# Gated linear recurrence heads: level decays as in-place products of blocks, heads interleaved

## The chip, the core and the metric

The kernel runs on one core of one Trainium2 chip. Time is the device time of one execution in microseconds (us). TensorE (PE) multiplies matrices, VectorE (DVE) does elementwise work and reductions, ScalarE (ACT) functions by table and copies, GpSimd (POOL) further elementwise work, and SyncE (SP) issues loads. Each engine runs its own program, and they meet only at semaphores. On-chip memory is SBUF; matmuls write PSUM, 8 banks of 128 partitions x 512 f32.

## The reference

A trunk of two layers, width 1024, 1024 tokens. Layer 0 has two mixers side by side, an S5 state space model with a gated linear unit (GLU) and an HGRN2 recurrence of 4 heads; layer 1 has sliding window attention. Each layer ends in an MLP and a gated embedding. The change is in the HGRN2 heads alone:

```python
log_f = jnp.logaddexp(jnp.log(jnp.maximum(lbf, 1e-30)),
                      jnp.log1p(-lbf) + jax.nn.log_sigmoid(zf))
k = (1.0 - lbf) * jax.nn.sigmoid(-zf)
...
def step(S, xs):                      # chunks of 64 tokens, 4 heads
    q_c, k_c, v_c, g_c = xs           # g_c is log_f
    b = jnp.cumsum(g_c, axis=2)
    o_inter = jnp.einsum('bhtk,bhkv->bhtv', q_c * jnp.exp(b), S)
    diff = b[:, :, :, None, :] - b[:, :, None, :, :]
    decay = jnp.exp(jnp.where(causal[None, None, :, :, None], diff, -jnp.inf))
    att = jnp.einsum('bhtk,bhtsk,bhsk->bhts', q_c, decay, k_c)
    o = o_inter + jnp.einsum('bhts,bhsv->bhtv', att, v_c)
    b_last = b[:, :, -1:, :]
    S_new = (jnp.exp(b_last[:, :, 0, :])[..., None] * S
             + jnp.einsum('bhsk,bhsv->bhkv', k_c * jnp.exp(b_last - b), v_c))
    return S_new, o
...
o = o * lax.rsqrt(jnp.mean(o * o, axis=-1, keepdims=True) + EPS) * head_norm.astype(f32)
o = o.reshape(bsz, L, HG_WIDTH) * jax.nn.silu(g.astype(f32))
```

The forget factor f is lb + (1 - lb) sigmoid(z), per token and per key channel (128 a head). A query at t meets a key at s <= t with the product of all factors between them.

## The kernel before

The projection writes forget logits, queries, values and gates of all heads to DRAM, channels on partitions and tokens along the row. SP loads them back a head at a time (L311 to L345). A head has 1024 tokens, in two halves of 512, each of four chunks of 128.

The pair (t, s) of a chunk is split by levels. At the level of width w, the query is in the right and the key in the left half of the same block of 2w tokens, and the decay is split at the middle of the block: one factor goes to the key and one to the query. Seven widths (64 to 1) and the diagonal cover the lower triangle. Before the change the factors come from logarithms: ScalarE takes the sigmoid by Exp, Ln and Exp (`sigmoid`, L1095) and the logarithm of f (`decay`), VectorE the cumulative sums by a scan (`cumulate`) and, per level, the differences to the block's middle (`level_exponents`, L1587 and L1588), ScalarE their exponentials (`level_exps`), and GpSimd multiplies them with keys and queries (`levels`, L466 and L467). TensorE then does eight 128x128 products per chunk (L732, L734) into two banks, and VectorE takes from each its part by a mask (L1617) and sums the eight (L1620). All ScalarE calls go through one helper, line L958; two-operand VectorE steps with a wait of their own through L1380.

Around this, per chunk: values and decayed keys are transposed (L723, L724) and copied by ScalarE; their product (L744) updates the state on VectorE (L1625, L1629); the state and the attention times values give the output (L752, L756), which ScalarE copies out. Per half the squares are summed by a matmul with ones (L760), and `mean_square`, `rstd_head`, `product`, `y_high` and `y_low` make the normed, gated output, split into two parts for the output projection.

The order of the work is written out by hand in each engine's `head`: while chunk c of one half is multiplied, the exponents of the next half are prepared. The heads are a hardware loop (Fori) of three and a last one. In front, the GLU of the S5 mixer takes four turns of ScalarE and VectorE (`for m in range(4)`), with the first half of head 0 prepared between them. After the heads SP restores the residual, and TensorE starts the output projection (`unit`, L539) when the last mid_lo is written.

Of the kernel before, what the change touches and what calls it, by code (L numbers as in the profile page):

```python
# [19 lines left out]
F32, F32R = mybir.dt.float32, mybir.dt.float32r  # L20
# [3 lines left out]
P = 128  # L24
# [10 lines left out]
LEVELS = [64, 32, 16, 8, 4, 2, 1]  # L35
# [40 lines left out]
def build(nc, a, out):  # L76
# [70 lines left out]
    QV = at("hg_qv", [P, 2, 2, HALF], F32, hg)  # L147
    G = at("hg_g", [P, T], F32, hg + 8 * K)
    LVL = at("hg_levels", [P, 2, 7, HALF], F32, hg + 12 * K)
    KK = at("hg_k", [P, 2, HALF], F32, hg + 40 * K)  # L150
    QB = at("hg_q_decayed", [P, 2, HALF], F32, hg + 44 * K)
    KD = at("hg_k_decayed", [P, 2, HALF], F32, hg + 48 * K)
    OUTH = at("hg_out", [P, 2, HALF], F32, hg + 52 * K)
    F = at("hg_f", [P, HALF], F32, hg + 56 * K)
    BC = at("hg_cumulative", [P, HALF], F32, hg + 58 * K)
    TA = at("hg_tmp_a", [P, HALF], F32, hg + 60 * K)
    TB = at("hg_tmp_b", [P, HALF], F32, hg + 62 * K)
    TC = at("hg_tmp_c", [P, HALF], F32, H_AT + 20 * K)
    TD = at("hg_tmp_d", [P, HALF], F32, H_AT + 22 * K)
    ENDS = at("hg_chunk_decay", [P, 2, HALF // P], F32, H_AT + 24 * K)  # L160
    MASK = at("hg_masks", [P, 8, P], F32, H_AT + 16 * K)
    MP = at("hg_masked", [P, 2, 8, P], F32, H_AT)
    PC = at("hg_gate", [P, T], F32, H_AT + 8 * K)
    PA = at("hg_squares", [P, HALF], F32, H_AT + 12 * K)
    PD = at("hg_product", [P, HALF], F32, H_AT + 14 * K)
    VK = at("hg_v_kd_tokens", [P, 2, 2, P], F32, H_AT + 28 * K)
    AT = at("hg_att", [P, 2, P], F32, H_AT + 30 * K)
    SS = at("hg_state", [P, P], F32, H_AT + 31 * K)
# [29 lines left out]
    with ctx:  # L198
# [14 lines left out]
        s5_y_done s5_y_copied s5_y_stored s5_ut_loaded lb_in lb_exp glu_tanh_in glu_tanh glu_zz glu_sig masks_ready  # L213
        hg_f_loaded hg_g_loaded hg_f hg_sigmoid_f hg_log_f hg_k_made hg_cumulated hg_to_end hg_exp_b hg_exp_end
        hg_level hg_level_exp hg_qv_scaled hg_decayed hg_levels hg_g_scaled hg_sigmoid_g hg_gate_made hg_tr
        hg_tr_copied hg_lvl_done hg_lvl_read hg_att hg_ds_done hg_state hg_o_done hg_o_copied hg_squares_made hg_ss
        hg_ss_read hg_rstd hg_y_ready hg_y_high hg_y_low dist_ready slopes_ready at_vt_done at_vt_copied at_qk_done
# [8 lines left out]
        hg_qv_loaded = [sem(f"hg_qv_loaded{i}") for i in range(2)]  # L226
# [13 lines left out]
        def _(sp):  # L240
# [78 lines left out]
            def hg_load(dst, hd, j, tokens, signal):  # L319

                sp.dma_start(dst, fqig_dram[bass.ds(hd * 4 * P + j * P, P), tokens]).then_inc(signal, 16)

            def f_load(hd, half):
                hg_load(F[:, :], hd, 0, slice(half * HALF, (half + 1) * HALF), S["hg_f_loaded"])

            def qv_load(hd, half):
                for j in range(2):
                    hg_load(QV[:, half, j, :], hd, 1 + j, slice(half * HALF, (half + 1) * HALF), hg_qv_loaded[half])

            f_load(0, 0)  # L330
            qv_load(0, 0)
            qv_load(0, 1)
            hg_load(G[:, :], 0, 3, slice(0, T), S["hg_g_loaded"])
            sp.wait_ge(S["hg_f"], 1)
            f_load(0, 1)
            with sp.Fori(1, HEADS) as hd:
                for half in range(2):
                    sp.wait_ge(S["hg_f"], hd * 2 + half)
                    f_load(hd, half)

# [1535 lines left out]
```

## Time and profile before

| | us |
|---|---|
| Median of 3 runs | 2933.19 (2929.24 to 2935.98) |
| Span of the profiled execution | 2922.3 |
| Around the span, to the median | 10.9 |
| Busy: TensorE / VectorE / GpSimd / ScalarE | 2578.5 / 1322.4 / 937.7 / 663.9 |
| Heads: last GLU turn to output projection | 438.9 to 715.9, 277.0 |

The span is from the first to the last instruction. The busy times overlap; over the whole program TensorE is at 88%, most of it the dense matmuls of L539, and the share of an engine says little of a stage. A group row gives the line, engine and operation, output and inputs, shapes, count, then busy us and mean ns of one, then idle us before it with what ended the idle time. A timeline row begins with start and length in us and ends with xcount; a length covers the whole run of xcount. A matmul in f32 leaves two records of 128x128.

### The profile page before, as it was taken

The numbers are of one execution on the slowest core, as the hardware profiler recorded it, in microseconds if no ns is written. First come the engines' busy times: TensorE is split into PE (matmuls) and PEld (weight loads), VectorE is DVE, ScalarE is ACT, GpSimd is POOL, SyncE is SP. The second block draws the span as 40 slices with busy tenths as digits, with TensorE's granted clock in tenths as the row PEclk, the third lists the DMA queues.
The fourth block names the chain that finished last, engine by engine and source line by source line (L and its number), as shares of the span: only waits on it lengthen the run. The fifth ranks groups of instructions, "written<-read, shape, count | busy, mean of one in ns | idle before, by whom it ended". The sixth has DMA issues, their size and how long they took to land.

```text
span 2922.3 us, 31974 instructions
## 1 busy us (share of the span) xinstructions
PE 2578.5 (88%) x11854; PEld 2104.6 (72%) x11854; DVE 1322.4 (45%) x1434; ACT 663.9 (23%) x1021; POOL 937.7 (32%) x629
## 2 busy tenths in 40 slices
PE   7988954456999999999999896669999999999997
PEld 5876734445888888888887684447888888888885
DVE  5778168886424323242452614553334242332635
ACT  3110056663220010101121203552210201101214
POOL 2322066652333333233332232222332332333230
PEclk9999576777999999999999897788999999999998
DMA  6352210001111111111121123101111111111111
GB/s 181 105 95 91 72 58 32 30 25 68 54 43 51 50 46 47 50 50 43 50 65 43 52 93 104 40 0 29 45 50 50 50 43 50 50 45 49 51 58 65
DMA packets 245356, 166.19 MB, mean 57 GB/s; under 512 B 14520, under 2 KB 230688, under 8 KB 245280
## 3 DMA queue, kind: packets, MB, share of 16 engines
q1 hardware_dynamic: 224160, 132.74, 15.8%
q10 hardware_dynamic: 21136, 32.64, 3.9%
q8 instruction: 39, 0.64, 0.1%
q14 instruction: 21, 0.17, 0.0%
HBM read 136.92 MB, written 27.26 MB: 56 GB/s over the span
## 4 chain that ended last, share of the span: by engine, by line
PE 74%; DVE 13%; ACT 6%; issue 4%; POOL 1%; DMA 1%; ACTq 0%; DVEq 0%; SPq 0%; POOLq 0%
PE ps L539 67%; ACT at_scores L958 1%; ACT L958 1%; PE ps L693 1%; DVE at_scores L1785 1%; DVE softmax_stats L1787 1%; PE ps L691 1%; DVE hg_levels L1588 1%; PE ps L606 1%; DVE s_ba L1380 1%; PE ps L835 1%; ACT mid_hi L958 1%; DVE s_tmp L1380 1%; DVE hg_levels L1587 1%; DVE hg_masked L1617 1%
## 5 line engine op out<-in xcount | busy, mean ns | idle before, releaser
L410 POOL CAST w_hi<-w_raw 128x1024 fp32r<-128x1024 f32 x198 | 211.6, 1069 | 1641.3 <-PE ps L539 1510.6
L539 PE MATMUL ps<-x_hi,w_hi 128*128 128x512 f32 x1760 | 546.2, 392 | 13.8 <-DVE stage L1371 11.5
L539 PE MATMUL ps<-x_lo,w_hi 128*128 128x512 f32 x1760 | 542.9, 390 | 0.0
L539 PE MATMUL ps<-x_hi,w_lo 128*128 128x512 f32 x1760 | 542.7, 390 | 0.0
L412 POOL TENSOR_TENSOR w_lo<-w_raw,w_hi 128x1024 fp32r<-128x1024 f32 x198 | 479.4, 2421 | 15.9
L539 PE MATMUL ps<-mid_hi,w_hi 128*128 128x512 f32 x1312 | 409.7, 394 | 30.5 <-DVE mid_lo L1546 17.5
L539 PE MATMUL ps<-mid_lo,w_hi 128*128 128x512 f32 x1312 | 407.3, 392 | 0.0
L539 PE MATMUL ps<-mid_hi,w_lo 128*128 128x512 f32 x1312 | 407.2, 392 | 0.0
L539 PEld LDWEIGHTS ps<-x_hi,w_hi 128*128 128x128 f32 x1760 | 330.5, 188 | 86.3 <-issue 16.8
L539 PEld LDWEIGHTS ps<-x_lo,w_hi 128*128 128x128 f32 x1760 | 330.9, 188 | 69.1
L539 PEld LDWEIGHTS ps<-x_hi,w_lo 128*128 128x128 f32 x1760 | 330.9, 188 | 69.1
L958 ACT ACTIVATE stage<-stage 128x1024 f32<-128x1024 f32 x68 | 72.2, 1062 | 1073.5 <-DVE stage L1699 932.7
L539 PEld LDWEIGHTS ps<-mid_hi,w_hi 128*128 128x128 f32 x1312 | 248.4, 190 | 86.5 <-issue 13.4
L539 PEld LDWEIGHTS ps<-mid_lo,w_hi 128*128 128x128 f32 x1312 | 249.0, 190 | 52.4
L539 PEld LDWEIGHTS ps<-mid_hi,w_lo 128*128 128x128 f32 x1312 | 248.3, 189 | 52.1
L1699 DVE TENSOR_SCALAR stage<-ps 128x1024 f32<-128x1024 f32 x48 | 58.8, 1225 | 284.8 <-PE ps L539 284.8
L1709 DVE TENSOR_TENSOR stage<-ps,rstd 128x1024 f32<-128x1024 f32 x48 | 58.8, 1225 | 282.2 <-PE ps L539 281.2
L1713 DVE TENSOR_TENSOR residual<-residual,stage 128x1024 f32 x48 | 156.8, 3266 | 7.3 <-DVE stage L1709 3.7
L958 ACT ACTIVATE x_hi<-residual,vectors (+1 forms) x48 | 55.2, 1151 | 337.5 <-DVEq L1686 153.2
L958 ACT ACT_TABLE_LOAD x72 | 92.4, 1283 | 156.4 <-DVE stage L1765 112.6
L1701 DVE TENSOR_TENSOR mid_lo<-stage,mid_hi 128x1024 f32 x48 | 58.8, 1225 | 121.4 <-ACT mid_hi L958 121.4
L519 POOL TENSOR_TENSOR at_scores<-at_scores,softmax_stats 128x1024 f32<-128x1024 f32 (+1 forms) x32 | 57.3, 1791 | 147.8 <-DVE softmax_stats L1797 147.8
(241 smaller groups left out, 2642.6 us busy)
## 6 DMA issues: line engine op xcount, KB each, us to landing
w_raw<-w_mlp_in_in SPq DMA_DIRECT2D x64, 512.0 KB, 4.0
w_raw<-w_mlp_out_in SPq DMA_DIRECT2D x64, 512.0 KB, 4.1
w_raw<-w_in_even_in SPq DMA_DIRECT2D x20, 512.0 KB, 4.6
fqig_dram<-stage ACTq DMA_DIRECT2D x16, 512.0 KB, 2.6
w_raw<-w_ple_gate_in SPq DMA_DIRECT2D x16, 512.0 KB, 4.0
w_raw<-w_qkv_odd_in SPq DMA_DIRECT2D x12, 512.0 KB, 3.8
qkv_dram<-stage ACTq DMA_DIRECT2D x12, 512.0 KB, 2.6
x_tokens<-x_in SPq DMA_DIRECT2D x8, 512.0 KB, 7.3
```

The costliest lines, as they stand in the source:

```text
L410: pool.tensor_copy(WH[:, b, :], RAW[:, b, :]).then_inc(S["w_hi_done"], 1)
L412: pool.tensor_tensor(WL[:, b, :], RAW[:, b, :], WH[:, b, :].bitcast(F32), ALU.subtract).then_inc(S["w_ready"], 1)
L519: pool.tensor_tensor(pr, pr, den, ALU.mult).then_inc(S["at_norm"], 1)
L539: ins = pe.matmul(acc[:, h, :], w[:, k, :], x[:, k0 + k, h * HALF:(h + 1) * HALF], start=(k == 0 and w is wh and x is xh), stop=(k == kts ...
L606: ins = pe.matmul(ACC[u][:, h, :], w[:, k, :], x[:, k, h * HALF:(h + 1) * HALF], start=(k == 0 and w is whs[u] and x is XAh), stop=(k == K ...
L691: pe.matmul(o, TOEP[:, g, :], U[:, g, :], start=True, stop=False)
L958: return act.activation(o, i, f, **kw)
L1380: own(tt(o, x, y, op))
L1699: dve.tensor_scalar(ST[0][:, :], flat(ACC[b]), 0.0, None, ALU.max).then_inc(S["acc_free"], 1)
L1701: tt(tile(XBl, i * 2 + b), ST[1][:, :], tile(XBh, i * 2 + b).bitcast(F32), ALU.subtract).then_inc(S["mid_ready"], 1)
L1709: tt(ST[0][:, :], flat(ACC[b]), RSTD[:, :], ALU.mult).then_inc(S["acc_free"], 1)
L1713: own(tt(h, h, ST[0][:, :], ALU.add))
```

## The change

`LEVELS` goes up, from width 1 to 64. f itself is used, no logarithm: ScalarE makes 1 - sigmoid and f with its Sigmoid table (`forget`). VectorE builds a tree of products of f over blocks of 2, 4, ..., 128 tokens (`block_decays`), and keys and queries are updated in place (`update`): after level l every key carries the decay to the end of its block of 2w, and every query that from its block's start. So the products of a level need only the small tiles above the diagonal of their blocks: TensorE multiplies, per half of 512 tokens, 16 tiles of 32x16 at l = 0; 16 of 32x16 and 16 of 32x32 at l = 1; 16 of 32x32 at l = 2 and 3; 16 of 16x16, 8 of 32x32 and 4 of 64x64 at l = 4, 5 and 6: 108 a half, 216 a head. The diagonal and the levels up to block 16 are merged by copies under a mask (`near`, `attend`; copy_predicated), the three wider ones are written at their own place in PSUM and copied by ScalarE (`direct_copy`). The masked copies and the sums of L1617 and L1620 are gone, as are the GpSimd products.

After the last level the keys carry the decay to the end of their chunk and the queries that from its start, as the state update and the output need them. That work of head h - 1, with its norm and gate, stands between the levels of head h, on each engine; so does the making of f, keys, decays and first queries of head h + 1. ScalarE's turn for a head is two key copies, the gate, six steps of `forget`, two squares, two value copies, a table load, four steps of rstd, two direct copies and two y_high; the gate's sigmoid brings the other table load. The heads are written out instead of looped, with two sets of buffers. GpSimd keeps the scaling of queries and of the gate input, and their gate product. The chunk's values are transposed a head ahead (`value_tokens`).

Most of the new code (`@@` headers and removed lines left out, the latter being the functions above):

```diff
-LEVELS = [64, 32, 16, 8, 4, 2, 1]
+LEVELS = 7
+SUB = 32
+STEPS = 2 * LEVELS
...
+            def head_load(hd):
+                p = hd % 2
+                    if hd >= 2:
+                        sp.wait_ge(S["hg_blocks"], 2 * (hd - 2) + half + 1)
+                        sp.wait_ge(S["hg_update"], (hd - 2) * STEPS + half + 1)
+                        sp.wait_ge(S["hg_level"], (hd - 2) * STEPS + 2 + half + 1)
+                        sp.wait_ge(S["hg_v_tr"], 2 * (hd - 2) + half + 1)
+                    for j, dst in enumerate((FR, QR, VR)):
+                        rows_ = slice((hd * 4 + j) * P, (hd * 4 + j + 1) * P)
+                        sp.dma_start(dst[:, p, half, :], fqig_dram[rows_, half * HALF:(half + 1) * HALF]).then_inc(hg_loaded[p][half], 16)
...
+            def level(hd, l, half):
+                p, u, step = hd % 2, 2 * hd + half, hd * STEPS + 2 * l + half
+                if l == 0:
+                    pe.wait_ge(S["hg_prep"], u + 1)
+                    if hd:
+                        pe.wait_ge(S["hg_near_read"], u - 1)
+                else:
+                    pe.wait_ge(S["hg_update"], step - 1)
+                if l == 4 and hd:
+                    pe.wait_ge(S["hg_direct_copied"], u - 1)
+                near, direct = PS[:, NEARS[half], :], PS[:, DIRECT[half], :]
+                k, q, qs = KS[:, p, half, :], QP[:, p, half, :], QR[:, p, half, :]
+                for c in range(4):
+                    t = c * P
+                    if l < 4:
+                        for j in range(4):
+                            rows, s = slice(SUB * j, SUB * (j + 1)), t + SUB * j
+                            if l < 2:
+                                ins = pe.matmul(near[rows, t + l:t + SUB:2], k[:, s:s + SUB], qs[:, s + l:s + SUB:2], start=True, stop=True)
+                            if l:
+                                ins = pe.matmul(near[rows, t + l * SUB:t + (l + 1) * SUB], k[:, s:s + SUB], q[:, s:s + SUB], start=True, stop=True)
+                    else:
+                        w = 1 << l
+                        for s in range(0, P, 2 * w):
+                            ins = pe.matmul(direct[s:s + w, t + s + w:t + s + 2 * w], k[:, t + s:t + s + w], q[:, t + s + w:t + s + 2 * w],
+                                            start=True, stop=True)
+                ins.then_inc(S["hg_level"], 1)
...
+            for hd in range(HEADS + 1):
+                now, tail = hd < HEADS, hd - 1
+                for l in range(LEVELS):
+                    for half in range(2):
+                        if now:
+                            level(hd, l, half)
+                        if hd and l == 0:
+                            key_tokens(tail, half)
+                        if hd and l == 1 and half == 1:
+                            state_steps(tail, 0)
+                        if hd and l == 2 and half == 0:
+                            state_steps(tail, 1)
+                        if hd and half == 1 and l in (3, 4):
+                            outputs(tail, l - 3)
+                            if now:
+                                value_tokens(hd, l - 3)
+                        if hd and half == 1 and l in (4, 5):
+                            head_squares(tail, l - 4)
...
+            def forget(hd, half):
+                u, p = 2 * hd + half, hd % 2
+                act.wait_ge(S["hg_z"], u + 1)
+                if hd >= 2:
+                    act.wait_ge(S["hg_k_tr"], u - 3)
+                fn(KS[:, p, half, :], FR[:, p, half, :], ACT.Sigmoid, scale=-1.0)
+                own(fn(TMP[:, half, :], FR[:, p, half, :], ACT.Sigmoid))
+                told(fn(FR[:, p, half, :], TMP[:, half, :], ACT.Identity, scale=keep[:, hd:hd + 1], bias=floor_[:, hd:hd + 1]), "hg_f_made")
...
+            def keys(hd, half):
+                k = KS[:, hd % 2, half, :]
+                dve.wait_ge(S["hg_f_made"], 2 * hd + half + 1)
+                dve.scalar_tensor_tensor(k, k, keep[:, hd:hd + 1], RSTD[:, half * HALF:(half + 1) * HALF], ALU.mult, ALU.mult)
+            def query_decay(hd, half):
+                u, p = 2 * hd + half, hd % 2
+                dve.wait_ge(S["hg_f_made"], u + 1)
+                dve.wait_ge(S["hg_q_scaled"], u + 1)
+                if hd >= 2:
+                    dve.wait_ge(S["hg_o"], u - 3)
+                told(tt(QP[:, p, half, :], QR[:, p, half, :], FR[:, p, half, :], ALU.mult), "hg_prep")
...
+            def block_decays(hd, half):
+                for l in range(LEVELS):
+                    pairs = blocks(hd, half, l).rearrange("p (n two) -> p n two", two=2)
+                    ins = tt(blocks(hd, half, l + 1), pairs[:, :, 0], pairs[:, :, 1], ALU.mult)
+                    if l < LEVELS - 1:
+                        own(ins)
+                told(ins, "hg_blocks")
+            def update(hd, l, half):
+                p, w, step = hd % 2, 1 << l, hd * STEPS + 2 * l + half
+                n = HALF // (2 * w)
+                k, q = (x[:, p, half, :].rearrange("p (n two w) -> p n two w", two=2, w=w) for x in (KS, QP))
+                d = blocks(hd, half, l).rearrange("p (n two) -> p n two", two=2)
+                dve.wait_ge(S["hg_level"], step + 1)
+                if l == 0:
+                    dve.wait_ge(S["hg_blocks"], 2 * hd + half + 1)
+                tt(k[:, :, 0, :], k[:, :, 0, :], d[:, :, 1:2].to_broadcast([P, n, w]), ALU.mult)
+                told(tt(q[:, :, 1, :], q[:, :, 1, :], d[:, :, 0:1].to_broadcast([P, n, w]), ALU.mult), "hg_update")
+            def near(hd, half):
+                s = PS[:, (4, 6)[half], :].rearrange("p (c l t) -> p c l t", l=4, t=SUB)
+                dve.wait_ge(S["hg_level"], hd * STEPS + 2 * 3 + half + 1)
+                for l in range(4):
+                    m = NEAR[:, l, :].bitcast(mybir.dt.int32).unsqueeze(1).to_broadcast([P, 4, SUB])
+                    ins = dve.copy_predicated(ATD[:, half, :, :], m, s[:, :, l, :])
+                    if l < 3:
+                        own(ins)
+                told(ins, "hg_near_read")
...
+            def attend(hd, half):
...
+                    d = ATD[:, half, c, :].unsqueeze(1).to_broadcast([P, 4, SUB])
+                    ins = dve.copy_predicated(AT[:, half, c * P:(c + 1) * P].rearrange("p (j t) -> p j t", t=SUB),
+                                              m.rearrange("p (j t) -> p j t", t=SUB), d)
+                told(ins, "hg_att")
...
+            for hd in range(HEADS + 1):
+                now, tail, nxt = hd < HEADS, hd - 1, hd + 1
+                for l in range(LEVELS):
+                    if now:
+                        for half in range(2):
+                            update(hd, l, half)
+                            if l == 3:
+                                near(hd, half)
+                    if hd and l == 0:
+                        for half in range(2):
+                            attend(tail, half)
+                    if hd and l in (1, 2):
+                        states(tail, l - 1)
+                    if nxt < HEADS and l == (1 if hd == 0 else 2):
+                        for half in range(2):
+                            forget_in(nxt, half)
+                    if hd and l in (4, 5):
+                        mean_square(tail, l - 4)
+                    if nxt < HEADS and l == 4:
+                        for half in range(2):
+                            keys(nxt, half)
+                            block_decays(nxt, half)
+                    if nxt < HEADS and l == 5:
+                        for half in range(2):
+                            query_decay(nxt, half)
+                if hd:
+                    for half in range(2):
+                        product(tail, half)
+                    for half in range(2):
+                        y_low(tail, half)
```

The instructions of VectorE in the middle of a head. Before, behind the sum of one chunk, exponents of the next half fill the time to the next chunk's products (hg_levels are these exponents, hg_cumulative the cumulative logs):

```order
L1620 TENSOR_REDUCE hg_att<-hg_masked 128x128 [waits hg_lvl_read]
L1623 ISA
L1625 COPY hg_state<-ps 128x128 [waits hg_ds_done]
L1587 TENSOR_TENSOR hg_levels<-hg_cumulative 128x4x64
L1588 TENSOR_TENSOR hg_levels<-hg_cumulative 128x4x64
L1587 TENSOR_TENSOR hg_levels<-hg_cumulative 128x8x32
L1588 TENSOR_TENSOR hg_levels<-hg_cumulative 128x8x32
L1587 TENSOR_TENSOR hg_levels<-hg_cumulative 128x16x16
L1588 TENSOR_TENSOR hg_levels<-hg_cumulative 128x16x16
L1587 TENSOR_TENSOR hg_levels<-hg_cumulative 128x32x8
L1588 TENSOR_TENSOR hg_levels<-hg_cumulative 128x32x8
L1617 TENSOR_TENSOR hg_masked<-ps,hg_masks 128x1024 [waits hg_lvl_done]
```

Now, at the levels 0 and 1 of a head in steady state (hg_keys and hg_queries are updated, hg_f and hg_block_decay are the tree, hg_att the attention of the head before):

```order
L1621 TENSOR_TENSOR hg_keys<-hg_keys,hg_f 128x256 [waits hg_blocks,hg_level]
L1622 TENSOR_TENSOR hg_queries<-hg_queries,hg_f 128x256
L1621 TENSOR_TENSOR hg_keys<-hg_keys,hg_f 128x256 [waits hg_blocks,hg_level]
L1622 TENSOR_TENSOR hg_queries<-hg_queries,hg_f 128x256
L1643 COPY_PREDICATED hg_att<-hg_same_block,hg_att_near 128x128 [waits hg_near_read,hg_direct_copied]
L1643 COPY_PREDICATED hg_att<-hg_same_block,hg_att_near 128x128 x3
L1643 COPY_PREDICATED hg_att<-hg_same_block,hg_att_near 128x128 [waits hg_near_read,hg_direct_copied]
L1643 COPY_PREDICATED hg_att<-hg_same_block,hg_att_near 128x128 x3
L1621 TENSOR_TENSOR hg_keys<-hg_keys,hg_block_decay 128x128x2 [waits hg_level]
L1622 TENSOR_TENSOR hg_queries<-hg_queries,hg_block_decay 128x128x2
L1621 TENSOR_TENSOR hg_keys<-hg_keys,hg_block_decay 128x128x2 [waits hg_level]
L1622 TENSOR_TENSOR hg_queries<-hg_queries,hg_block_decay 128x128x2
```

Each update waits for TensorE's tiles of its own level and half, and the masked copies of the head before stand between the levels.

VectorE at the mean square. Before, it follows a state step and is followed by exponents:

```order
L1620 TENSOR_REDUCE hg_att<-hg_masked 128x128 [waits hg_lvl_read]
L1623 REGISTER_ALU
L1629 SCALAR_TENSOR_TENSOR hg_state<-hg_state,hg_chunk_decay,ps 128x128 [waits hg_state,hg_ds_done]
L1591 REGISTER_ALU
L1594 TENSOR_SCALAR hg_product<-ps 128x512 [waits hg_ss]
L1587 TENSOR_TENSOR hg_levels<-hg_cumulative 128x4x64
```

Now it stands after level 4, and the keys and the tree of the next head stand behind it (hg_rstd is the mean square's output):

```order
L1621 TENSOR_TENSOR hg_keys<-hg_keys,hg_block_decay 128x16x16 [waits hg_level]
L1622 TENSOR_TENSOR hg_queries<-hg_queries,hg_block_decay 128x16x16
L1621 TENSOR_TENSOR hg_keys<-hg_keys,hg_block_decay 128x16x16 [waits hg_level]
L1622 TENSOR_TENSOR hg_queries<-hg_queries,hg_block_decay 128x16x16
L1667 TENSOR_SCALAR hg_rstd<-ps 128x512 [waits hg_ss]
L1587 SCALAR_TENSOR_TENSOR hg_keys<-hg_keys,one_minus_lb,rstd 128x512 [waits hg_f_made]
L1607 TENSOR_TENSOR hg_block_decay<-hg_f 128x256
L1607 TENSOR_TENSOR hg_block_decay<-hg_block_decay 128x128 [waits dve_step]
```

The wait for hg_ss is one for the ones-matmul of the head before; the update of level 5 comes after the tree.

TensorE. Before, a chunk is two transposes, eight full products, then the state product and the output of the chunk before:

```order
L723 MATMUL ps<-identity,hg_qv 128x128 [waits hg_tr_copied]
L724 MATMUL ps<-identity,hg_k_decayed 128x128
L732 MATMUL ps<-hg_levels 128x128 [waits hg_lvl_read]
L732 MATMUL ps<-hg_levels 128x128 x6
L734 MATMUL ps<-hg_qv,hg_k 128x128
L742 ISA [waits hg_tr_copied]
L744 MATMUL ps<-hg_v_kd_tokens 128x128 [waits hg_state]
L756 MATMUL ps<-hg_att,hg_v_kd_tokens 128x128 [waits hg_att,hg_o_copied]
```

Now, from level 3 to level 4 of a head, the outputs of the head before and the next transposes stand between two levels:

```order
L712 MATMUL ps<-hg_queries,hg_keys 32x32 [waits hg_update]
L712 MATMUL ps<-hg_queries,hg_keys 32x32 x15
L758 MATMUL ps<-hg_att,hg_v_tokens 128x128 [waits hg_att,hg_states]
L757 MATMUL ps<-hg_queries,hg_state 128x128
L758 MATMUL ps<-hg_att,hg_v_tokens 128x128
L757 MATMUL ps<-hg_queries,hg_state 128x128
L758 MATMUL ps<-hg_att,hg_v_tokens 128x128
L757 MATMUL ps<-hg_queries,hg_state 128x128
L758 MATMUL ps<-hg_att,hg_v_tokens 128x128
L736 MATMUL ps<-identity,hg_v 128x128 [waits hg_k_copied,hg_loaded10]
L736 MATMUL ps<-identity,hg_v 128x128 x3
L716 MATMUL ps<-hg_queries,hg_keys 16x16 [waits hg_direct_copied,hg_update]
```

Between the 32x32 tiles of level 3 and the 16x16 tiles of level 4 come seven full products and four transposes.

## Rows read from the trace of the kernel before

**Rows 1.** Windows: busy us and count per engine, granted clock, DMA; three stretches.

```profile
core 0: us, PE busy (x) PEld busy (x) DVE busy (x) ACT busy (x) POOL busy (x), PEclk, DMA share, GB/s
177.50:190.00 12.50, 12.50 (x253) 12.19 (x253) 1.60 (x10) 4.83 (x9) 0.00 (x0) 1.00 0.01 3
300.00:346.00 46.00, 46.00 (x149) 35.03 (x149) 0.00 (x0) 3.58 (x6) 0.00 (x0) 0.50 0.11 23
438.90:715.90 277.00, 136.02 (x768) 120.76 (x768) 225.48 (x280) 168.90 (x256) 155.21 (x139) 0.72 0.07 23
```

**Rows 2.** Timeline at both ends of the heads: start us, us, engine, line, [idle before].

```profile
438.93 0.47 PE L723 MATMUL ps<-identity,hg_qv 128*128 128x128 f32 x1 [13.86 <-DVEq L1657]
...
441.98 3.25 DVE L1662 TENSOR_TENSOR mid_lo<-stage,mid_hi 128x1024 fp32r<-128x1024 f32 x1 [1.12 <-ACT mid_hi L958]
...
715.94 1.22 PE L539 MATMUL ps<-mid_hi,w_hi 128*128 128x512 f32 x2 [6.37 <-DVE mid_lo L1610]
```

**Rows 3.** Groups of instructions by shape, 438.9 to 715.9 us, all engines.

```profile
L958 ACT ACT_TABLE_LOAD x49 | 62.9, 1283 | 1.7 <-ACT hg_tmp_c L958 0.6
L1620 DVE TENSOR_REDUCE hg_att<-hg_masked 128x128 f32<-128x1024 f32 x32 | 61.4, 1919 | 1.1
L1617 DVE TENSOR_TENSOR hg_masked<-ps,hg_masks 128x1024 f32<-128x1024 f32 x32 | 38.9, 1217 | 18.6 <-PE ps L734 18.6
...
L958 ACT ACTIVATE hg_levels<-hg_levels 128x512 f32<-128x512 f32 x49 | 30.0, 629 | 42.5 <-DVE hg_levels L1588 42.0
...
L450 POOL TENSOR_TENSOR hg_qv<-hg_qv,rstd 128x512 f32<-128x512 f32 x14 | 19.0, 1375 | 0.0
...
L479 POOL TENSOR_TENSOR hg_gate<-hg_gate,hg_g 128x1024 f32<-128x1024 f32 x4 | 9.6, 2398 | 9.1 <-ACT hg_gate L958 9.1
...
L1629 DVE SCALAR_TENSOR_TENSOR hg_state<-hg_state,hg_chunk_decay,ps 128x128 f32<-128x128 f32 x24 | 8.1, 338 | 0.0
...
L1594 DVE TENSOR_SCALAR hg_product<-ps 128x512 f32<-128x512 f32 x8 | 5.5, 690 | 3.2 <-PE ps L760 3.2
```

**Rows 4.** Timeline of VectorE with GpSimd idle, then busy, and a copy.

```profile
465.11 0.42 DVE L1587 TENSOR_TENSOR hg_levels<-hg_cumulative 128x256 f32<-128x256 f32 x1
465.44 0.42 DVE L1588 TENSOR_TENSOR hg_levels<-hg_cumulative 128x256 f32<-128x256 f32 x1
...
471.44 0.96 DVE L1588 TENSOR_TENSOR hg_levels<-hg_cumulative 128x256 f32<-128x256 f32 x1
472.07 0.91 POOL L466 TENSOR_TENSOR hg_levels<-hg_levels,hg_k 128x256 f32<-128x256 f32 x1
472.31 0.95 DVE L1587 TENSOR_TENSOR hg_levels<-hg_cumulative 128x256 f32<-128x256 f32 x1
...
534.59 0.28 DVE L1625 COPY hg_state<-ps 128x128 f32<-128x128 f32 x1
```

**Rows 5.** Group of VectorE's operations on 16 elements, whole span.

```profile
L1380 DVE TENSOR_TENSOR s_phase<-s_phase 128x16 f32<-128x16 f32 x36 | 6.3, 175 | 1.2
```

**Rows 6.** Timeline of TensorE: small tiles of the S5 stage, full tiles of the heads.

```profile
177.46 0.26 PE L656 MATMUL ps<-s_c,s_bbar 64*16 64x16 f32 x4
177.58 0.54 PE L658 MATMUL ps<-s_ca,s_bbar 64*16 64x112 f32 x4
...
212.49 3.77 PE L676 MATMUL ps<-s_u,s_end_weights 128*64 128x128 f32 x64
...
288.49 1.22 PE L693 MATMUL ps<-s_state,s_ca 64*128 64x127 f32 x4
...
439.41 3.19 PE L732 MATMUL ps<-hg_levels 128*128 128x128 f32 x14
...
466.23 1.73 PE L732 MATMUL ps<-hg_levels 128*128 128x128 f32 x14
```

**Rows 7.** Timeline of ScalarE: first and last of the GLU's four sigmoids.

```profile
406.23 1.11 ACT L958 ACTIVATE stage<-ps,vectors 128x1024 f32<-128x1024 f32 x1
...
437.36 1.12 ACT L958 ACTIVATE stage<-ps,vectors 128x1024 f32<-128x1024 f32 x1
```

More of the change, by code:

```diff
@@ L156, in build @@
[L156 to L164, printed above, removed]
@@ L483, in _ @@
-            keys_and_queries(0, 0, first=True)
-            levels(0, 0)
+                pool.tensor_tensor(PC[:, hd % 2, :], PC[:, hd % 2, :], G[:, :], ALU.mult).then_inc(S["hg_gate_made"], 1)
+            queries(0)
+            gate_scale(0)
             one(22, 22)
             one(23, 24)
-            with pool.Fori(0, HEADS - 1) as hd:
-                heads_chunks(hd, False)
-            heads_chunks(HEADS - 1, True)
+            for hd in range(HEADS):
+                gate_mult(hd)
+                if hd < HEADS - 1:
+                    queries(hd + 1)
+                    gate_scale(hd + 1)
@@ new lines, in outputs @@
+            def outputs(hd, half):
+                u = 2 * hd + half
+                pe.wait_ge(S["hg_states"], u + 1)
+                pe.wait_ge(S["hg_att"], u + 1)
+                for c in range(4):
+                    o, t = PS[:, OB[half], c * P:(c + 1) * P], slice(c * P, (c + 1) * P)
+                    first = half == 0 and c == 0
+                    if not first:
+                        pe.matmul(o, SS[:, half, c, :], QP[:, hd % 2, half, t], start=True, stop=False)
+                    ins = pe.matmul(o, VT[:, half, t], AT[:, half, t], start=first, stop=True)
+                ins.then_inc(S["hg_o"], 1)
@@ new lines, in states @@
+            def states(hd, half):
+                u = 2 * hd + half
+                dve.wait_ge(S["hg_ds"], u + 1)
+                if half:
+                    dve.wait_ge(S["hg_states"], u)
+                ends = blocks(hd, half, LEVELS)
+                for c in range(4 - half):
+                    ds = PS[:, half, c * P:(c + 1) * P]
+                    nxt = SS[:, half, c + 1, :] if c < 3 else SS[:, 1, 0, :]
+                    if half == 0 and c == 0:
+                        ins = dve.tensor_copy(nxt, ds)
+                    else:
+                        ins = dve.scalar_tensor_tensor(nxt, SS[:, half, c, :], ends[:, c:c + 1], ds, ALU.mult, ALU.add)
+                    if c < 3 - half:
+                        own(ins)
+                told(ins, "hg_states")
```

467 lines of the change are left out of this document (188 added, 279 removed).

## The prediction

> **What bounds the kernel now.** I read the views in this order: the windows, the timeline at both ends of the heads, the groups of instructions by shape, and single stretches of the timeline for the pace of one operation.
>
> The windows give the stage: the four heads take from 438.9 to 715.9 us, 277 us, 69 us each, and in them VectorE is busy 225.5 us (81%), ScalarE 168.9, GpSimd 155.2, TensorE 136.0 at a granted clock of 0.72 [rows 1]. No other engine is above 61%. The ends come from the timeline: the first transpose waits 13.86 us for VectorE's queue, VectorE leaves the gated linear unit (GLU) at 445.2, and the output projection starts at 715.94 after waiting for the last mid_lo of VectorE [rows 2]. All later work hangs on that matmul, so what the heads save comes off the end in full.
>
> The groups say what VectorE does there: the masked copy of the eight level products, 32 times 1.217 us, and the sum over them, 32 times 1.919, together 100 of its 225 us [rows 3]. ScalarE spends 62.9 us on 49 table loads [rows 3]. So VectorE bounds, with exchanges between four engines in the other 19%.
>
> **The change part by part.** Removed are the masked copies and sums (100.3 us of VectorE), the level exponents, scans and clamps, the exponentials and logarithms with nearly all table loads, and GpSimd's 56 level products. Added are updates of keys and queries in place, the small level matmuls, and the merging of near blocks. VectorE, per head in the middle of the pipeline:
> - 28 updates of 128x256. A pair in the trace starts 0.33 us apart, though each lasts 0.42 [rows 4]. 28 x 0.34 = 9.5. The broadcast operand and the stride are those of the subtraction now in that row.
> - 16 predicated copies, no such operation in the trace. Below, an operation of 16 elements takes 0.175 [rows 5], so 2.8 per head; above, one of 128x512 takes 0.69 [rows 3], so 11. The nearest row is the copy of 128x128, 0.28 [rows 4]; with a third operand I take 0.30, so 4.8.
> - 7 state steps at 0.338 [rows 3]: 2.4.
> - 14 operations of 128x512 (forget 2, keys 2, query 2, mean square 2, product 4, y_low 2) at 0.70, rounded up from 0.690 [rows 3]: 9.8.
> - 14 block decays, each waiting for the one before: two at 0.42, two at 0.30, ten at 0.18 and 0.3 of drains, between the rows of 256 and of 16 elements [rows 4, 5]: 3.6 with the drains.
>
> That is 30.1 us. GpSimd still does four things a head: two scalings of 1.375, and a scaling and the gate, both 128x1024, of 2.4 each [rows 3], 7.5 us. While it runs, VectorE's pair starts 0.87 us apart instead of 0.34 [rows 4], so at most 7.5 x 0.61 = 4.6 is lost and at least nothing, if GpSimd falls on waits or on reads of PSUM. I take 2.5: 32.6 us.
>
> Then VectorE's waits for TensorE. The halves alternate: while one half is updated the other is multiplied. A level of 16 matmuls a half takes 1.2 us (below) against 0.68 of VectorE, and the tail of the head before has to fill the difference. At level 1 there are 32 matmuls a half and four state steps ahead of them, and attend ran before: about 1.7 us is left. At level 2, three more state steps: 0.7. At level 4 the mean square stands behind output matmuls, four transposes and a ones-matmul: 8 x 0.33 + 4 x 0.16 + 1.3 = 4.6, of which updates cover 1.1: 3.5. Together 5.9, and **38.5 us a head**. Behind the mean square in VectorE's queue stand the next head's keys and block decays, for which that head's first matmuls wait; since these come three levels later, the wait is paid once, not twice.
>
> TensorE, per head: 216 level matmuls. The nearest rows are four records, two matmuls, of 64x16, which start 0.12 us before the next line's, and 64 records of 128x64 in 3.77 us [rows 6]; a matmul leaves two records. Below: 0.06 each, 13 us. Above: a matmul of 128 columns takes 3.19 / 7 = 0.46 at the lower clock [rows 6], a quarter of it for 32 columns is 0.11, 24 us. I take 0.075, near the lower end, because the fixed part and not the columns should rule: 16.2. 22 full matmuls at 0.33, between 1.73 / 7 = 0.25 and 0.46 [rows 6]: 7.3. 16 transposes, one record where a matmul has two [rows 2], at 0.16: 2.6. Two ones-matmuls of 512 columns, four times a full one (1.0 to 1.8), at 1.4: 2.8. Sum 28.9, from 22 to 42: under VectorE's 32.6 as I choose, above it at the upper end.
>
> ScalarE: 20 operations of 128x512 at 0.629, a gate of 1.1 and two table loads of 1.283 [rows 3]: 16.3 us, under half of the period, so it is no bound. GpSimd with 7.5 is none either. Loads are double buffered, and the stage's DMA share is 0.07 [rows 1]: they stay hidden, and if not, forget_in would be late first.
>
> Head 0 has no tail to carry: 9.5 + 2.4 (near, 8 copies) + 1.4 + 1.4 + 3.6 + 1.4 (next head's forget, keys, decays, queries) = 19.7, waits for the bare levels 4, contention 1: 25. The tail after head 3 overlaps with nothing: attend 2.4, states 1.3, outputs 4.9, squares 0.6, ones-matmul 1.4, mean 0.7, rstd 1.3, product 1.4, y_high and y_low 1.3: 15.4, with hand-overs 18. The stage is 25 + 3 x 38.5 + 18 = 158.5.
>
> The GLU in front also changes. Its four sigmoids run from 406.23 to 437.36, 10.4 us a turn [rows 7], because ScalarE changes tables twice a turn and VectorE's level work sits between. The turn itself is sigmoid 1.1, VectorE 2.2, copy 1.1, subtraction 1.2, about 6.5 with hand-overs; tables no longer alternate. With near_masks (2.6) ahead and the first sigmoid at 403, VectorE is free at about 431 rather than 445.2.
>
> **Sum:** 431 + 158.5 = 589.5 against 715.9: 126.4 less. The profiled span of 2922.3 becomes 2796; 10.9 us lie around it to the median of 2933.2, which gives 2807 us.
>
> The Trainium skill (VectorE: DVE Perf Modes, The TRN2 errata — SBUF-src ops pay a fixed extra latency per instruction) speaks against many narrow operations: each pays a fixed cost, (N+151)/0.96, which for 256 elements is an estimate of 0.42 us. The duration in the row agrees to the digit, but the starts 0.33 apart [rows 4] show part of the fixed cost overlapped. By the rule updates would cost 28 x 0.42 = 11.8, 2.3 more a head and 9 us in all; by the row, what the sum has.
>
> **The rivals.** *TensorE sets the pace.* For it: the clock was 0.72 in the stage and 0.50 through 46 us of sparse matmuls [rows 1], and the small tiles leave the array mostly idle. A head is then 41.3 of work (23.8 + 3.7 for transposes + 10.1 + 3.7, all at the upper ends) and 8 to 9 of exchanges at levels that nothing overlaps, 50; 431 + 30 + 150 + 22 = 633, 83 less: 2850. Against: at 177.5 to 190 the clock was 1.00 with tiles as small [rows 1].
>
> *VectorE without waits.* The tail of the head before, some 17 us of VectorE's work, may cover every wait: 33.5 a head, 428 + 23 + 100.5 + 15 = 566.5, 149 less: 2784. Against: the mean square's place.
>
> *Slower: small tiles cost as in the S5 stage.* There, matmuls of 64x127 between ones of another shape take 1.22 / 4 = 0.305 a record, 0.6 a matmul [rows 6]. With that 216 x 0.6 = 130, and 12 of full ones: 142 a head; 431 + 4 x 142 + 15 = 1014, 298 more: 3231. It decides from a period of (715.9 - 431 - 15) / 4 = 67, that is (67 - 12) / 216 = 0.25 us a level matmul. Against: 3.77 us for 64 records and the 0.12 for four [rows 6] are far below.
>
> The Trainium skill (TensorEngine Tiling (Array Packing), Key Properties) says that a change of tiling mode drains TensorE; the new order alternates 16, 32, 64 and 128 wide tiles some 20 times a head. The trace has one place for it and one against it [rows 6], and the chance of this rival is no higher for it.
>
> *It hardly moves the time*, because a transfer or the fetch of the longer, unrolled program becomes the wait: nothing in the trace speaks for it; near 2933.
>
> **Chances.** Forecast 0.60, TensorE sets the pace 0.22, no waits 0.12, slower 0.04, hardly any change 0.02 (half of it counted as faster). The forecast's terms alone move it from 2795 (no contention, less waiting) to 2825 (copies at 0.5, full contention). The range of 2780 to 2850 takes in the two neighbours and leaves out the far side of TensorE's case. Faster by over 0.2%, about what a measurement can tell from no change: 0.95; within 0.2%: 0.01; slower: 0.04.
>
> **What would show it.** Right: the projection's first matmul near 590; VectorE busy over 80% of about 158 us; updates of 0.42 us starting 0.34 apart; predicated copies near 0.3; level matmuls at about 0.04 a record; VectorE idle before the mean square only. Wrong: records of small matmuls over 0.06 or TensorE busy throughout with VectorE waiting at each update (the second case), copies at 0.7, a GLU turn still near 10 us, or idle time before forget_in put down to a DMA.

## The result, and the profile after

The changed kernel takes 2777.57 us (median of 4, 2776.14 to 2779.11) against 2932.83 before: 0.9469 of it, 95% interval 0.9458 to 0.9481, or 155.3 us less. The forecast was 2807, its range 2780 to 2850.

The windows of the kernel after, cut at the first update of each head, at the last head's own tail and at the output projection (columns as in [rows 1]; the first four rows are heads 0 to 3 with the tail of the head before, the fifth is the bare tail of head 3):

```profile
434.02:459.60 25.58, 10.34 (x403) 8.72 (x404) 24.86 (x56) 5.64 (x10) 7.41 (x4) 0.50 0.26 84
459.60:493.95 34.35, 21.51 (x535) 17.41 (x533) 31.50 (x81) 14.70 (x24) 8.94 (x4) 0.80 0.19 63
493.95:527.74 33.79, 21.05 (x496) 17.28 (x496) 31.32 (x80) 15.22 (x24) 9.01 (x4) 0.75 0.06 18
527.74:551.01 23.27, 16.96 (x433) 13.78 (x433) 21.04 (x61) 11.52 (x18) 3.83 (x1) 0.87 0.01 3
551.01:566.55 15.54, 9.52 (x49) 7.75 (x49) 9.56 (x24) 6.48 (x10) 0.00 (x0) 0.72 0.00 0
```

VectorE (third busy figure) fills over 90% of each head and 62% of the bare tail; TensorE has 21 us of work in 34. The whole is 132.5 us where 158.5 were forecast. The last head takes 23.3, not a steady 34. The groups and the timeline of VectorE after, as answers to [rows 3, 4]:

```profile
L1630 DVE COPY_PREDICATED hg_att_near<-hg_near_masks,ps 128x128 f32<-128x128 int32 x32 | 9.6, 299 | 0.8
...
L1643 DVE COPY_PREDICATED hg_att<-hg_same_block,hg_att_near 128x128 f32<-128x128 int32 x32 | 6.9, 303 | 0.0
...
L1667 DVE TENSOR_SCALAR hg_rstd<-ps 128x512 f32<-128x512 f32 x8 | 5.5, 689 | 8.1 <-PE ps L765 8.1
```

```profile
495.29 1.72 DVE L1643 COPY_PREDICATED hg_att<-hg_same_block,hg_att_near 128x128 f32<-128x128 int32 x8
496.90 0.42 DVE L1621 TENSOR_TENSOR hg_keys<-hg_keys,hg_block_decay 128x256 f32<-128x256 f32 x1
497.24 0.42 DVE L1622 TENSOR_TENSOR hg_queries<-hg_queries,hg_block_decay 128x256 f32<-128x256 f32 x1
...
500.75 1.48 DVE L1622 TENSOR_TENSOR hg_queries<-hg_queries,hg_block_decay 128x256 f32<-128x256 f32 x1
502.15 1.49 DVE L1621 TENSOR_TENSOR hg_keys<-hg_keys,hg_block_decay 128x256 f32<-128x256 f32 x1
...
513.65 0.69 DVE L1667 TENSOR_SCALAR hg_rstd<-ps 128x512 f32<-128x512 f32 x1 [1.21 <-PE ps L765]
```

Updates start 0.34 apart, as forecast; while GpSimd scales the queries (500.5 to 503.4) they start 1.4 apart. GpSimd in the same stretch:

```profile
496.73 3.81 POOL L456 TENSOR_TENSOR hg_gate<-hg_gate,hg_g 128x1024 f32<-128x1024 f32 x1 [24.32 <-ACT hg_gate L981]
500.51 2.84 POOL L448 TENSOR_TENSOR hg_q<-hg_q,rstd 128x512 f32<-128x512 f32 x2
```

Not all of its work slows VectorE. Beside the gate product (496.7 to 500.5) the updates keep their 0.34, and it is GpSimd that takes 3.81 us for what takes 2.4 alone; beside the scalings GpSimd keeps its pace (1.4 each), and each of the two updates ends about 0.3 us after a scaling. In these rows one of the two waits for the other's instruction; they do not share evenly. Copies under a mask (predicated copies) last 0.30, but eight in a row take 1.72, since they overlap where none waits for the last. The only idle time of note is 1.21 before a mean square.

TensorE's small tiles, in the same head and at the same clock as full products (one record of two each):

```profile
502.29 0.46 PE L712 MATMUL ps<-hg_queries,hg_keys 128*32 128x32 f32 x32 [1.94 <-DVE hg_queries L1622]
...
510.27 0.49 PE L757 MATMUL ps<-hg_queries,hg_state 128*128 128x128 f32 x2
510.59 0.39 PE L758 MATMUL ps<-hg_att,hg_v_tokens 128*128 128x128 f32 x2
510.81 0.39 PE L757 MATMUL ps<-hg_queries,hg_state 128*128 128x128 f32 x2
```

Sixteen tiles take 0.46 us, 0.03 each; full products start 0.22 apart. Both stretches have a granted clock of 1.00. Of the products of the other half in this head, those from 505.3 to 507.0, at 0.50, start 0.43 apart. Over the whole head the 216 tiles keep TensorE busy for 10.4 us, 0.048 each.

### The profile page after: what moved, and what is told of

Read it like the earlier page. It is cut to its first block, busy times and chain, and to the rows that moved or that the text cites. A ratio compares the mean times of both kernels' runs of the same rounds, so it can differ in the third digit from the quotient of the medians.

```text
span 2776.1 us, 33670 instructions
## 1 busy us (share of the span) xinstructions
PE 2527.9 (91%) x13070; PEld 2052.9 (74%) x13070; DVE 1223.5 (44%) x1457; ACT 534.7 (19%) x833; POOL 804.7 (29%) x485
## 4 chain that ended last, share of the span: by engine, by line
PE 79%; DVE 12%; ACT 4%; issue 3%; DMA 1%; ACTq 0%; DVEq 0%; SPq 0%; POOLq 0%; POOL 0%
PE ps L516 71%; ACT at_scores L981 1%; PE ps L670 1%; DVE at_scores L1849 1%; DVE softmax_stats L1851 1%; PE ps L668 1%; PE ps L583 1%; DVE s_ba L1385 1%; PE ps L858 1%; DVE s_tmp L1385 1%; DVE s_ca L1385 1%; DVE hg_keys L1621 1%; DVE hg_queries L1622 1%; ACT mid_hi L981 1%; PE ps L949 1%
## 5 line engine op out<-in xcount | busy, mean ns | idle before, releaser
L516 PEld LDWEIGHTS ps<-mid_hi,w_hi 128*128 128x128 f32 x1312 | 247.8, 189 | 81.9 <-issue 10.9
L1323 DVE SCALAR_TENSOR_TENSOR x_lo<-residual,vectors,x_hi (+1 forms) x40 | 58.1, 1452 | 64.7 <-ACT x_hi L981 64.7
```

The source lines that it names most:

```text
L516: ins = pe.matmul(acc[:, h, :], w[:, k, :], x[:, k0 + k, h * HALF:(h + 1) * HALF], start=(k == 0 and w is wh and x is xh), stop=(k == kts ...
L1323: dve.scalar_tensor_tensor(tile(XAl, m), tile(H, m), COLS[:, bass.ds(m + g, 1)], tile(XAh, m).bitcast(F32), ALU.mult, ALU.subtract).then_i ...
```

## The experiments

In all of them the median and a comparison with the kernel before on the same chip were taken; differences below are to the 2777.6 of the changed kernel, or for variants of the kernel before to its median in the same runs. The median of the kernel before lay between 2932.3 and 2935.3 us in these comparisons, so a difference of 3 to 4 us is near the smallest that they can tell.

**Is the last head short for want of the next one's work?** `last_full` adds, in the last head only, products of 128x512 at levels 2, 4 and 5 and a chain of seven halvings per half at level 4:

```diff
+                    if nxt == HEADS and l in (2, 4, 5):
+                        spare_work(l)
```

> The last head gets idle work on VectorE where the others prepare the next head: six products of 128x512 and two chains of seven halvings. Theory (the last head is short because this work is missing, and VectorE sets its pace): 7.8 to 8.5 us more, near 2786. Rival (the last head is short for another reason, such as TensorE's clock of 0.87 there, and has room): no change, 2778.

Measured 2784.70, 7.1 more. Its last head runs from 527.86 to the copies of its own attend, 31.4 us instead of 23.3 (timeline of VectorE in `last_full`):

```profile
545.85 1.84 DVE L1676 TENSOR_TENSOR hg_sigmoid<-hg_sigmoid 128x256 f32<-128x256 f32 x7
...
559.23 0.90 DVE L1643 COPY_PREDICATED hg_att<-hg_same_block,hg_att_near 128x128 f32<-128x128 int32 x4
```

The theory holds: on VectorE that work is on the path.

**Does TensorE have room?** `mm2` and `mm4` put each level matmul in a loop of 2 or 4:

```diff
-                                ins = pe.matmul(near[rows, ...
+                                for _ in range(2):
+                                    ins = pe.matmul(near[rows, ...
```

> Every level matmul is issued twice, the second over the first. Theory (a small tile costs about its columns, near 0.035 us, and TensorE has room beside VectorE): 216 x 0.035 = 7.6 us more of TensorE a head, most of it hidden; about 2 us a head come through where a level waits bare, 8 us in all, 2785 (2780 to 2795). Rival, the price of my forecast (0.075 a tile, 28.9 us of TensorE a head): 45 a head, TensorE sets the pace, about 11 more in each of four heads, 2820 or more.

> Every level matmul is issued four times. Theory (0.035 us each): 23 us more of TensorE a head, which with the 21 it has goes past VectorE's 33.8: about 12 more a head in steady state, more where levels are bare, 50 to 60 in all, near 2830. Rival (0.075 each): 49 more a head, some 150 to 170 in all, 2930 to 2950.

Measured 2802.24 (+24.7) and 2891.82 (+114.2): both between the two expectations. One steady head of each, `mm2` then `mm4`:

```profile
507.80:546.35 38.55, 29.80 (x928) 26.42 (x928) 30.97 (x80) 15.55 (x24) 7.66 (x4) 0.82 0.05 17
```

```profile
549.80:608.60 58.80, 51.85 (x1800) 48.38 (x1798) 29.18 (x80) 15.61 (x24) 7.15 (x4) 0.97 0.04 13
```

The first doubling adds 8.8 us to TensorE's busy time in this head, 0.041 a tile, and 4.8 us to its length; the next 432 tiles add 22.1 us busy, 0.051 each, and 20.3 us of length. So a tile costs 0.04 to 0.05, not 0.075 (the granted clock rises with the tiles, 0.75, 0.82, 0.97, so this is no price at one clock), and the kernel as it stands is short of TensorE's bound but not far: I had taken three quarters of the doubled work as hidden, and more than half of it comes through. The likely reason, that the levels of a half are a chain of TensorE and VectorE, was not tried apart.

**What does GpSimd cost VectorE?** `nopool` replaces its scaling of queries and gate input and its gate product by empty instructions (the output lacks them), three times as here:

```diff
-                pool.tensor_tensor(G[:, :], G[:, :], RSTD[:, :], ALU.mult).then_inc(S["hg_g_scaled"], 1)
+                pool.nop().then_inc(S["hg_g_scaled"], 1)
```

> GpSimd's scaling of queries and gate inputs and its gate product are left out (the output then lacks them). Theory (GpSimd slows VectorE while it runs; in the trace 3.7 to 3.8 us in each of the heads 1 and 2, 6.3 in head 0, 0.3 in head 3): 14 us less in the heads, near 2764. Rival (the slow stretches have another cause, such as the loads that run then): no change, 2778.

Measured 2760.72, 16.9 less. Head 0 falls from 25.6 to 20.6 us, heads 1 and 2 from 34.35 and 33.8 to 30.9 and 30.25, and 3.1 us come off the GLU ahead of them. The same two updates of head 2 that started 1.4 apart start 0.34 apart, though the loads still run, so the rival is out:

```profile
489.02 0.42 DVE L1622 TENSOR_TENSOR hg_queries<-hg_queries,hg_block_decay 128x256 f32<-128x256 f32 x1
489.36 0.42 DVE L1621 TENSOR_TENSOR hg_keys<-hg_keys,hg_block_decay 128x256 f32<-128x256 f32 x1
```

**How much is the interleaving?** `seq` takes it out: each head's tail after its own levels, on TensorE, VectorE and ScalarE.

```diff
-                    if hd and l == 0:
-                        for half in range(2):
-                            attend(tail, half)
+                for half in range(2):
+                    attend(hd, half)
```

> The in-place levels stay, the interleaving goes: each head's key transposes, states, outputs, norm and gate come after its own last level (the next head's preparation stays between the levels). Theory (the tail of 15.5 us alone, and levels of 23 to 25.6 alone, hide nothing of each other): three heads of 41 instead of 33.9, and the last of 17 + 15.5 instead of 23.3 + 15.5: 15 to 24 us more, 2793 to 2802. Rival (VectorE's work is the same and the waits are small anyway): up to 5 more, 2783.

Measured 2788.82, 11.3 more, between the two; a steady head takes 36.6 to 37.0 us. So 144 of the 155 us come without the interleaving of the tail, from the in-place levels with their shorter preparation (the next head's preparation is still between the levels here).

**What bounded the heads before?** Three variants of the kernel before. `before_no_merge`:

```diff
-                    told(dve.tensor_reduce(AT[:, b, :], MP[:, b, :, :].rearrange("p l t -> p t l"), X, ALU.add), "hg_att")
+                    told(dve.tensor_copy(AT[:, b, :], MP[:, b, 0, :]), "hg_att")
```

and the same for the masked copy ahead of it (from one level's 128x128 of PSUM). `before_tables`:

```diff
             def head(hd, last):
+                act.preload_act_table_set("natural_log_exp_and_others")
```

and one more ahead of the loop. `before_both` has both edits.

> The kernel before, with its masked copy (1.22 us) and sum (1.92 us) per chunk each replaced by a copy of 128x128 (0.28 us); the attention is then not the right one. Theory (VectorE bounds the heads before): 32 x (1.22 + 1.92 - 2 x 0.25) = 84 us less of VectorE, most of it off the time, 2855 (2848 to 2870). Rival (the exponents' path over ScalarE with its table loads and GpSimd, 155 to 169 us busy, and the exchanges take over): 45 us less, 2888, and the rest of what the change gained is due to the shorter path on those two.

> The kernel before, with one table set that holds both Exp and Ln, loaded once a head (the heads' table loads go from 49 to 5, 56 us of ScalarE). Theory (two paths of nearly equal length in the heads, VectorE's own work and the chain of VectorE, ScalarE and GpSimd that makes the levels): removing one of them leaves the other, 20 to 35 us less, near 2905. Rival (ScalarE's path alone set the pace): 50 us less, 2883. Rival of my prediction (VectorE alone): 0 to 10 less.

> The same, and the masked copy and the sum are each replaced by a copy of 128x128, so that the attention is not the right one. Theory (two paths): both shortened gains more than the two alone added, 80 to 100 us less, near 2843. Rival (the paths are in series, each gives its own): the sum of the two, 25 plus what the tables give, near 2880.

Measured 2908.28 (25.1 less), 2902.61 (32.7 less) and 2880.33 (55.0 less). The first edit took less from VectorE than the 84 us that I had worked out: the copy that stands for the sum took 0.53 us and not 0.25, the level exponents took 7 us more than before, and VectorE's busy time over the heads fell by 67 us, from 225.5 to 158.8. These 67 us gave 25; taking 42 of 49 table loads, 54 us, from ScalarE gave 33, and both together the sum, 58, within 3. In `before_both` the level exponents take 85.7 us on VectorE instead of 63.3, so part of what was saved there went again. My theory of two parallel paths fell, and that of VectorE alone too. What fits is a ring of exchanges, in which each piece counts in part; it is read from these three times and the waits below, and not tried further. A window of `before_no_merge` that holds the heads up to 7 us before its output projection (at 698.01), and its waits there (us in total, times, longest):

```profile
438.90:691.00 252.10, 132.89 (x768) 119.92 (x768) 155.99 (x276) 166.62 (x254) 152.22 (x141) 0.72 0.08 25
```

```profile
POOL hg_q_decayed L456 <- ACT hg_chunk_decay L958: 73.3, 7, 12.0
DVE hg_masked L1617 <- PE ps L734: 50.9, 16, 6.2
...
PE ps L723 <- ACT hg_v_kd_tokens L958: 44.4, 11, 15.2
PEld ps L732 <- POOL hg_levels L467: 29.6, 4, 7.8
```

VectorE is busy 156 us of 252 and nobody more than 167 (up to 698.0 it is 159 of 259, and 170): every engine waits for another one.

**Pieces of VectorE's path after.** `ms_later` takes the mean squares at levels 5 and 6; `copies` lets the near copies of the halves alternate and makes attend's four copies one; `silu` makes the gate in one function of ScalarE and leaves GpSimd's product out:

```diff
-                    if hd and l in (4, 5):
-                        mean_square(tail, l - 4)
+                    if hd and l in (5, 6):
+                        mean_square(tail, l - 5)
...
-                    ins = dve.copy_predicated(ATD[:, half, :, :], m, s[:, :, l, :])
-                    if l < 3:
-                        own(ins)
+                    for half in range(2):
+                        if l:
+                            dve.wait_ge(own.sem, base + 2 * (l - 1) + half + 1)
+                        ins = dve.copy_predicated(ATD[:, half, :, :], m, view[half][:, :, l, :])
...
-                told(fn(PC[:, hd % 2, :], G[:, :], ACT.Sigmoid), "hg_sigmoid_g")
+                told(fn(PC[:, hd % 2, :], G[:, :], ACT.Silu), "hg_sigmoid_g")
```

> VectorE takes the mean squares one level later (5 and 6 instead of 4 and 5). Theory (VectorE is idle 1.21 us ahead of the first mean square in each of three heads, and the updates of level 5 cover it): 3.6 us less, 2774. Rival (the idle time moves to the product, which waits for the root of ScalarE): no change, 2778, or 1 us more.

> The near copies of both halves alternate, so that none waits for the one before it, and the four masked copies of attend are one of 128x512 per half. Theory (VectorE's instruction count sets the pace): near from 2.6 to 1.8 us a head, attend from 1.7 to 1.3: 1.2 x 4, 4 to 5 us less, 2773. Rival (levels behind are TensorE's chain, and the time goes into waits at level 4): no change.

> ScalarE makes the gate's silu in one function instead of a sigmoid, and GpSimd's gate product (2.4 us alone, 3.8 beside VectorE) is left out. Theory (GpSimd costs VectorE what it overlaps): a third of what leaving out all GpSimd work gave (16.9 us), 4 to 6 us less, 2773. Rival (silu brings a table of its own, four more loads of 1.28 us a head in ScalarE's queue ahead of the next head's forget factors): no gain or 1 to 5 us more.

Measured 2774.08 (3.5 less), 2773.58 (4.0 less) and 2773.90 (3.7 less, though five more table loads stand in ScalarE's queue). Then `best`, the first two, and `best_silu`, all three:

> After the change, the later mean square and the alternating copies together. Theory (VectorE's queue sets the pace and both take from it): the sum, 3.5 + 4.0 = 7.5 us less, 2770. Rival (TensorE's chain of levels takes over): 4 us less, 2773.5.

> These two and the gate by one silu function. Theory: again the sum, 11.2 us less, 2766. Rival: as with best, the third gives nothing more.

Measured 2772.12 (5.5 less, between the two) and 2766.47 (11.1 less, the sum). The last is the fastest version with the whole output, 0.9425 of the kernel before (interval 0.9409 to 0.9441).

These steps are small beside the differences between comparisons: the kernel before took 2933.05 in that of `ms_later`, 2933.39 in that of `copies` and `silu`, 2935.30 in that of `best` and `best_silu`. Taken each from its own kernel before, the gains over the changed kernel are 3.7, 4.6 and 4.2, then 7.9 for `best` and 13.6 for `best_silu`, against sums of 8.3 and 12.5. In the traces the output projection starts 2.7, 1.9 and 3.0 us earlier, then 6.1 and 9.2. So that the gains add is likely, that `best` falls short is not shown, and neither is the exact size of a single one.

**The time around the span.** `before_again` is the kernel before, unchanged.

> The kernel before, unchanged, for span and time of each execution. If the 10.9 us between the profiled span and the median were a fixed piece around the program, each execution shows about 11 between its own time and span. Rival: each execution shows 1 to 2 us, as after the change, and the profiled one was simply 9 us quicker than the median.

Measured 2933.33. Its profiled execution took 2932.93 with a span of 2931.2: 1.7 us around it, and so the rival holds. That the first profiled execution was some 9 us quicker is inferred from this: its own time is not on record. Its output projection starts at 722.12 us, 6.2 later than in [rows 2].

## Why the prediction was wrong

The mechanism that I forecast held in the main: VectorE sets the pace after the change (`last_full`: 7.8 us of added work, 7.1 in the time), and the time fell. TensorE counts beside it, since more than half of its added work comes through in `mm2`. The size missed by 29.4 us, and by terms it divides so:

- **The last head was charged as a steady one**: the step "The stage is 25 + 3 x 38.5 + 18". Head 3 prepares no next head: my own terms for that (forget, keys, decays, queries: 1.4 + 1.4 + 3.6 + 1.4) are 7.8 us. It took 23.3, so this step cost 15.2 us: the 7.8 of missing work (`last_full` gives 7.1 to 8.1), 2.2 of contention that head 3 escapes (in the trace 0.3 against the 2.5 taken), and the rest the waits and copies below.
- **VectorE's waits for TensorE**, put at 5.9 a head, were 1.5 in head 2: 0.3 where I had 2.4 at the levels 1 and 2, 1.21 where I had 3.5 at the mean square. Two steps failed. One is the price of TensorE: 0.075 a tile against 0.048, ones-matmuls at 1.4 against 1.07, and the outputs ahead of the mean square at 0.33 against 0.23, so that their chain took 3.4 us and not 4.6 (the outputs of the other half did take 0.36, but VectorE was busy meanwhile). The other is the overlap: I let updates cover 1.1 us of that chain (four of them at my own 0.34 are 1.4), and near copies and updates cover 2.2. 3.4 - 2.2 is the 1.2 measured. `ms_later` speaks for it being on the path: heads 1 and 2 are 1.2 us shorter there. Heads 1 and 2 came out at 34.35 and 33.8 for 38.5, 8.9 us together.
- **The tail** was 15.5, the sum without the hand-overs that I added: 2.5 us. Head 0 was 25.6 for 25.
- **The distance from span to median**: I carried 10.9 us over to the changed kernel, as if fixed. It was 1.5 there and 1.7 in `before_again`; the profiled execution of before was itself some 9 us quicker than the median. 9.4 us.
- Against these, VectorE came free of the GLU at 434.0 instead of 431, 3.0 us; in `nopool`, without GpSimd's work, they come back (430.96). And what follows the heads took 3.1 us more than in the profile of before (2209.5 against 2206.4), though no more than in `before_again` (2209.1).

15.2 + 8.9 + 2.5 - 0.6 + 9.4 - 3.0 - 3.1 = 29.3.

Of the other terms, updates (0.34) and block decays (3.5 a head) were right; full operations started 0.60 to 0.72 apart for the 0.70 taken, and predicated copies were 4.0 for 4.8. Contention with GpSimd was 3.5 a head by `nopool`, midway between the 2.5 taken and the upper end of 4.6; single updates took 1.5 us under it, more than the 0.95 of [rows 4].

Taken as a price from start to start, the rule of a fixed cost per instruction (the Trainium skill, VectorE: DVE Perf Modes, The TRN2 errata — SBUF-src ops pay a fixed extra latency per instruction) puts updates 0.42 apart, an estimate. One update does last 0.42, but they start 0.34 apart, and the measurement decides. `copies`, which has fewer and wider instructions, gained 4.0 us, but it also takes waits out between the near copies, so it does not test the rule. Of the drain at a change of tiling mode (the Trainium skill, TensorEngine Tiling (Array Packing), Key Properties) the trace shows 0.1 us at the one place looked at: the first 128x128 product behind sixteen 16x16 tiles (510.27) starts 0.32 before the next, against 0.22 in a row.

Of the rivals, "VectorE without waits" was nearest, 2784 with 33.5 a head, and it had the last head wrong in the same way. That its sum puts the projection at 566.5, where it started (566.55), is luck: the three later heads were taken 9.1 us too long, the GLU's end and head 0 8.6 too early and short, and the tail 0.5 too short. "TensorE sets the pace" fell; `mm4` shows where it begins. What I said of the kernel before, that VectorE bounds it, was wrong, and it did not show in the number because the sum was built from the new instructions and not from what was removed. Had I subtracted VectorE's 100 us of merging, I would have been misled: three quarters of them gave 25.

What stays open: of the 221 us that are left in the heads of `before_both`, how much each removed operation held was not tried one by one.

## What to carry to other kernels

Price the pipeline's last turn apart: it lacks the work for a next one, and its own tail is bare. Where the engines of a stage are between 49% and 81% busy, as here, the busiest need not be the bound: leave out its largest group once and see, for here 67 us less of its busy time gave 25. And compare spans with spans: the difference of one span and a median of other executions is no constant.

## What the runs showed of the hardware

More TensorE work raised its clock. In head 0, levels alone, the granted clock was 0.50 (1.2 GHz) with TensorE busy 10.3 of 25.6 us; in `mm2` 0.70, in `mm4` 0.97 with 41.4 of 54.7 busy. What the clock gave back cannot be read from the busy times alone: for one, two and four times the tiles they are 10.3, 18.2 and 41.4 us, the last four times the first at nearly twice the clock, and why is open. Within one head it moves too: in head 2 of the changed kernel it was 1.00 from 504.0 to 505.1 us and 0.50 from 505.1 to 508.5.

```profile
434.00:467.40 33.40, 18.21 (x801) 17.02 (x802) 23.31 (x56) 5.66 (x10) 7.35 (x4) 0.70 0.21 66
```

```profile
436.30:491.00 54.70, 41.42 (x1724) 40.01 (x1719) 22.10 (x56) 5.01 (x8) 6.33 (x4) 0.97 0.14 43
```

A 128x32 tile at 0.029 us, sixteen in a row, is cheaper than a quarter of a full product (0.22 / 4 = 0.055) at the same clock; over the head, with all sizes and the breaks between them, a tile cost 0.048. And asking for a table set that holds both Exp and Ln took the kernel before from 49 table loads in its heads to 7, 32.7 us for one line written twice.
